# Unread TensorE products in the mixers of a hybrid decoder step

## The reference

```
h = rmsnorm(x);  z = h @ w_in                      # 1024 -> 3756 columns
o_dn, o_rw, o_rt = deltanet(z), rwkv7(z), retention(z)
x = x + concat(o_dn, o_rw, o_rt) @ w_out
x = x + swiglu(rmsnorm(x))     # layer 0: dense, 2816 hidden
                               # layer 1: 8 experts, the best 2 of a token, 3584 hidden each
```

```
T = inverse(I + strictly_lower(products of keys))  # 64 x 64 in each chunk and head
u = u0 - w @ S;   o = q @ S + (q k) @ u;   S = decay * S + k @ u     # chunk after chunk
```

## Time and profile before

| | |
|---|---|
| device time, median of 3 runs | 1882.61 us (1880.7 to 1884.41) |
| the profiled execution | span 1869.9 us from first to last instruction; its device time is not on the page, the median stands 12.7 us above the span |
| mean granted clock of TensorE | 0.968 |
| VectorE busy | 470.3 us (25%) |
| ScalarE busy | 249.2 us (13%) |
| GpSimd busy | 91.3 us (5%) |

### The profile page before, as it was taken

The page is one execution under the profiler, slowest core; times in us unless marked ns, Lnnn a source line. Parts: engine busy times, 40 slices in busy tenths (PEclk is TensorE's granted clock), DMA queues, the critical chain, the costliest instruction groups (busy, mean ns, idle before and its releaser), DMA issues.

```text
span 1869.9 us, 38456 instructions
## 1 busy us (share of the span) xinstructions
PE 1808.4 (97%) x17710; PEld 981.9 (53%) x17710; DVE 470.3 (25%) x1039; ACT 249.2 (13%) x570; POOL 91.3 (5%) x118
## 2 busy tenths in 40 slices
PE   8999899999999999989989999999999999999997
PEld 6778875666666677887562333333333333333332
DVE  2436655200000343565641001001100100110031
ACT  2342222100000234222210000000000000000001
POOL 0000012100000000001310000000000000000000
PEclk9999897999999899989879999999999999999999
DMA  7330012723330433001199999999999999999992
GB/s 244 102 105 3 3 66 65 302 113 136 133 125 1 131 101 106 2 3 67 65 362 379 396 407 411 409 421 414 407 414 402 422 402 421 415 409 415 413 415 96
DMA packets 66663, 453.62 MB, mean 243 GB/s; under 512 B 10208, under 2 KB 37152, under 8 KB 42048
## 3 DMA queue, kind: packets, MB, share of 16 engines
q1 hardware_dynamic: 60704, 431.43, 57.6%
q0 software_dynamic: 5376, 19.49, 2.8%
q10 hardware_dynamic: 416, 0.16, 0.0%
HBM read 441.47 MB, written 9.60 MB: 241 GB/s over the span
## 4 chain that ended last, share of the span: by engine, by line
PE 93%; DVE 5%; ACT 1%; issue 1%; DMA 0%; DVEq 0%; SPq 0%; ACTq 0%
PE bank L541 91%; PE bank L545 2%; DVE ring L1373 1%; DVE work L1373 1%; DVE hT L1373 1%; DMA X<-x_in_dram 0%; DVE X L1373 0%; DVE work L1376 0%; DVE hT L1776 0%; DVE AV L1708 0%; ACT ring L2315 0%; DVE hT L1800 0%; ACT work L2339 0%; ACT L2228 0%; ACT L2318 0%
## 5 line engine op out<-in xcount | busy, mean ns | idle before, releaser
L541 PE MATMUL bank<-ring,hT 128*32 128x512 f32 (+2 forms) x6336 | 626.3, 538 | 0.7 <-DVE hT L1373 0.7
L541 PEld LDWEIGHTS bank<-ring,hT 128*32 128x32 f32 (+1 forms) x6336 | 223.5, 112 | 401.3 <-issue 388.3
L541 PE MATMUL bank<-hT,ring 128*128 128x288 f32 x1632 | 408.7, 411 | 2.4 <-DVEq L1426 2.4
L541 PE MATMUL bank<-ring,work 128*32 128x512 f32 (+4 forms) x3168 | 390.8, 569 | 0.0
L541 PEld LDWEIGHTS bank<-hT,ring 128*128 128x128 f32 x1632 | 311.3, 192 | 100.6 <-issue 13.8
L1373 DVE TENSOR_TENSOR work<-work,bank 128x384 f32<-128x384 f32 (+2 forms) x142 | 78.1, 560 | 766.1 <-ACT work L2460 502.7
L541 PEld LDWEIGHTS bank<-ring,work 128*32 128x32 f32 (+3 forms) x3168 | 129.5, 116 | 238.4 <-issue 235.3
L2460 ACT ACTIVATE work<-bank 128x512 f32<-128x512 f32 (+1 forms) x48 | 26.1, 544 | 549.9 <-PE bank L541 549.9
L541 PE MATMUL bank<-ring 64*64 64x64 f32 (+11 forms) x1152 | 78.3, 287 | 5.3 <-DVE SS L1373 2.7
L2224 ACT ACTIVATE ring<-bank 128x32 f32<-128x32 f32 (+7 forms) x144 | 41.5, 335 | 193.2 <-PE bank L541 168.6
L541 PEld LDWEIGHTS bank<-ring 64*64 64x64 f32 (+6 forms) x1152 | 54.9, 146 | 20.0 <-issue 13.0
(11 more groups left out here) (257 smaller groups left out, 1026.5 us busy)
## 6 DMA issues: line engine op xcount, KB each, us to landing
ring<-moe_dram SPq DMA_DIRECT2D x168, 2048.0 KB, 10.8
ring<-ffn_dram SPq DMA_DIRECT2D x22, 1536.0 KB, 12.7
ring<-w_in_dram SPq DMA_DIRECT2D x18, 1536.0 KB, 6.5
ring<-w_out_dram SPq DMA_DIRECT2D x2, 1536.0 KB, 7.3
work<-w_out_dram SPq DMA_DIRECT2D x2, 1280.0 KB, 7.8
ring<-w_out_dram SPq DMA_DIRECT2D x2, 1280.0 KB, 10.4
ring<-w_in_dram SPq DMA_DIRECT2D x2, 1152.0 KB, 5.3
C<-consts_dram SPq DMA_DIRECT2D x1, 1912.5 KB, 16.0
```

The lines of the kernel that those rows point to most:

```text
L541: return nc.tensor.matmul(out, lhsT, rhs, start=start, stop=stop, skip_group_check=True)
```

## The change

A function `beats(pe, n)` issues n products of the identity with a 128 x 128 constant, both already in SBUF, into the bank that the next `fill` will take, after waiting until that bank is free. Nobody reads them: the fill that follows overwrites them. They are called at fixed places of the mixers: ahead of waits, inside the trains of sample reads (after every second sequence), and after each group of 8 crossings. In `first_level` three such products go into the bank just taken. No other engine's stream is touched, and no wait is removed.

```diff
+        def beats(pe, n):
+
+            b, turn = len(fills) % 8, len(fills) // 8
+            pe.wait_ge(bank_free[b], turn)
+            for _ in range(n):
+                mm(pe, banks[b][:, 0:P], ident, cst("ones64"))
...
                 b, full = fill(pe, l, y, "L0", t)
+                if y == 0 and t == 0:
+                    for _ in range(3):
+                        mm(pe, b[:, 0:P], ident, cst("ones64"))
                 wait(pe, first_T, l, 3 * y + t)
...
                 for lev in range(1, 6):
                     tiles = [t for t in range(3) if lev < LEVELS[t]]
+                    if lev == 3:
+                        beats(pe, 3 if y else 6)
...
                 TT = inverse_memory(t)[0]
+                if y and t == 2:
+                    beats(pe, 2)
                 freed(pe, l, y, "XT", t, LEVELS[t] - 1)
...
                 if y:
+                    if t == 2:
+                        beats(pe, 1)
                     freed(pe, l, "XV", t)
...
                 if c:
+                    if y and c == 3:
+                        beats(pe, 3)
                     freed(pe, l, y, "W", c)
                     wait(pe, S_ok, l, y * 4 + c - 1)
...
                     before_u()
+                    if not y:
+                        beats(pe, (0, 2, 4, 4)[c])
                     wait(pe, U_ok, l, y * 4 + c - 1)
...
                         i = mm(pe, out, SS[s, p, q, :], both)
+                    if q % 2:
+                        beats(pe, 1)
                 i.then_inc(full, 1)
                 beside()
+                if not y:
+                    beats(pe, 2)
                 wait(pe, USO_ok, l, y)
...
                 i.then_inc(full, 1)
+                beats(pe, 3)
                 wait(pe, U_ok, l, y * 4 + 3)
...
             def sample_state(l, y, p):
+                if y == 0 and p == 2:
+                    beats(pe, 5)
                 wait(pe, UX_ok, l, y * 3 + p)
...
                             i = mm(pe, b[s, DS * x:DS * (x + 1)], SSr[k4, x, :], rt_qd[k4, DS * x:DS * (x + 1)])
+                        beats(pe, 1)
...
                 outputs_of_group(pe, l, 1)
+                beats(pe, 2)
                 wait(pe, Os_ok, l, 1)
```

## The result

The changed kernel takes 1890.15 us (median of 16 runs, 1885.84 to 1895.06), the kernel before, run beside it, 1879.86 (16 runs, 1871.61 to 1885.95): a ratio of 1.0057, 95% interval 1.0043 to 1.0071. The forecast of 1874.7 was wrong in its sign, and the time lies above its range.

The account below looks back on a forecast made before the run. TensorE, busy in 97% of the span, was taken to bound the kernel. Regained clock of 19.0 us, less 8.1 for open products and 3.0 for those at low clock, gave 7.9 off 1882.6: 1874.7 us, range 1862 to 1887.

Parts of the forecast that it names:

- The price of an open product: Unread product outside any wait on TensorE: 0.214 us at full clock; 19 a layer, 8.1 us in both layers.
- the 3.0 for low clock: In or behind the trains: seven products a layer cost double at half clock, 3.0 us over both layers.
- How much low time goes: In the mixers: 44.3 of 68.1 us at half clock disappear, worth 19.0 us.
- The signs of being wrong: Mixers: over 43 us or under 10 us at half clock, or open products of 0.38 us each, would refute it.
- 811.10: Second-layer time taken as the same place as the first layer's 1.57 us wait before 206.22, with a clock fall behind.
- The 12.7 us between the profiled span and the median: Whole kernel: runs' median stands 12.7 us above the 1869.9 span; kept unchanged in the forecast.
- the 0.43 us per low microsecond: Mixers: each microsecond at half clock loses 0.43 us, so all 68.1 are worth 29.3 us at most.
- products in waits: Mixers: most products lie in waits at least as long and cost nothing at full clock.
- the exception at the third sample state: Before the third sample state, five products wait for the bank VectorE's addition frees: 1.07 us on the path per layer.
- The third: Slower by overfilled waits behind the trains: 1896.0 at worst, 1889 if half true, if under 25.8 low us go; chance 0.13.
- The second rival: Only waits count, products in trains change nothing: 10.3 us gained, 8.1 and about 4 paid, 1884.4 us; chance 0.15.

Follow-up runs that it names:

- trains alone: Only the 12 products a layer in sample trains and crossings, added to the kernel before: 1894.49 us, ratio 1.0100.
- late waits alone: Kernel before plus only the 13 products a layer in waits behind the trains (last chunk's reads, sample transposes, means): 1872.17 us, ratio 0.9954.
- The kernel with the free bank: Changed kernel's 35 products a layer in waits, plus the five before the third sample state put into an already emptied bank: 1865.52 us, ratio 0.9928 to before.
- the wide pairs: 35 wait products a layer plus, at 12 places a layer in the trains, a pair of 64x64 products of 256 columns: 1885.22 us, ratio 1.0021 to before.
- waits alone: Changed kernel less 20 products a layer (trains, crossings, third tile, before third sample state), keeping 35 in waits: 1870.53 us, ratio 0.9952 to before.

## Why the prediction was wrong, step by step

**The price of an open product failed.** The step took 0.214 us from the projection's rate by columns and held 0.384 as the other bound. In a train it is 0.41 at full clock, above even that bound, and 0.72 at half. The rate came from a row in which weight loads of one shape follow each other beside the matmuls; among tiles of another shape neither bound held. In a group the products come near that rate (the five at 246.72 take 1.32 us, 0.26 each). Put as one price for the change of tile and one for each product, 0.41 for one and 1.32 for five give 0.18 and 0.23 us, an estimate: the rate was nearly right, and the change of tile, which the prediction put at nothing, was not. For trains and crossings the sum had 24 x 0.214 = 5.1 us, plus a share of the 3.0 for low clock; the runs have 13.6. All terms for products came to 8.1 + 3.0 = 11.1 us and measured 21.6: 10.5 of the miss.

**How much low time goes failed.** The step let 44.3 of 68.1 low microseconds go, for 19.0 us; the runs have 25.7, for 11.1 us: 7.9 of the miss. Right in it, by the profile, were the stretches behind the long waits. Wrong was that products in trains and crossings would cut each fall to 3.4: trains alone show no low time gone at all. In the changed kernel's train the clock fell 2.2 us after the first tiny product (209.26 to 211.50), with the second product just under way; in the kernel before it took 2.8 (210.92 in the earlier trace rows, 213.75 in the earlier trace rows).

The two together make 18.4 us, against 18.2 between the -7.9 forecast and the +10.3 measured. With 0.33 in place of 0.43 the first would be 7.9 and the second 10.5, so which of the two weighed more isn't shown.

**The signs of being wrong came true.** The prediction named low stretches of more than 43 us in the mixers, and the profile has 57; and open products of 0.38 each, where they take 0.41. The train of sample reads, for which it had 3.9 us, runs 6.1 up to its last product (209.26 to 215.37).

**One place was misread.** The prediction called 811.10 the same place as in the first layer. It lies behind a wait of 1.15 us that ends at 810.30, one chunk earlier than the 1.57 at 206.22. And the second layer's own wait of 1.63 us, which ends at 784.77, was followed by no fall in the same trace (1.00 from 784 to 800). So such a wait does not always bring the clock down.

**The span's surroundings were misread.** The 12.7 us between the profiled span and the median were taken as what lies around the span. In every run that is listed with its span, the two differ by 1.7 to 1.9 us. Of the other 10.9, 6.7 are that the profiled execution had little low time, 119.7 us at a clock of 0.968, against 135.2 in the median run, and 2.7 that the first three runs had a median of 1882.6 against 1879.9 for sixteen; 1.5 stay open. Only the 2.7 shifted the base, but a quick run's trace had also been the measure of how long the falls last.

**Right were** the 0.43 us per low microsecond, within 0.33 to 0.44; that products in waits cost next to nothing (0.05 each); and the exception at the third sample state, whose wait stayed (1.25 against 1.35) with the products behind it, 1.32 us where 1.07 had been worked out. Of the reason given for the 0.43, that waits and drains don't shorten, the trace of before shows the part on waits: 0.56 us before 299.58 at half clock, 0.55 before 904.61 in the second layer at full. No run here shows it of drains.

**The rivals.** The third named 1889 to 1896, and the time fell there by luck, for the road was another: it had the products in the waits behind the trains overfill them, while these are the ones that pay (late waits alone, 0.9954). The point that it gave, under 25.8 low microseconds gone, counted those of the mixers alone, where the profile has 11; and with the open products priced as they were, 21.6 / 0.43 = 50 would have had to go. The second rival came from the rule in the Trainium skill's page "TensorE: Matmul & The Clock Gate", section "Why this matters for your kernels", that idle time lets the clock drop. On its conclusion, that products in the trains are cost alone, it was right, as trains alone show; its price was too low by the same step as mine. On the cause the trace still differs: the clock fell inside trains without a pause.

**Not explained:** a new fall of 3.35 us at 249.00, just behind the late five products and the 32x512 products. The kernel with the free bank has none there. But the late waits (first row) and the wide pairs (second row), which don't have the five, do have one behind the same 32x512 products, so the five are not needed for it:

```profile
245.75:249.10 3.35, 3.35 (x70) 0.50 0.58 235
...
243.50:246.80 3.30, 3.30 (x68) 0.50 0.60 236
```

## What to carry to other kernels

Fill the waits that come after the clock has fallen, not the trains in which it falls. In this kernel work in a wait was covered, and behind the trains it brought low time down, while in a train it was paid in full and brought none. A filler needs a buffer that is free before the wait begins, not one that the same event frees. Price an added instruction among neighbours of its own shape and of others separately, and read what a clock change costs over many runs rather than from the one that was profiled.

## What was not expected of the hardware

A lone 128x128 fp32 product between 64x64 tiles takes 0.41 us at full clock, one in a group of its kind 0.26, and a pair of 64x64 tiles that moves 128 columns through each 0.25. And one and the same kernel runs with very different amounts of low clock: the twelve runs with waits alone range from a mean clock of 0.966 to 0.978, and from 1880.54 to 1860.22 us.
